# Late modulation products of a hybrid attention and mLSTM trunk, taken out of the attention steps and placed between tiles of the gate and branch projections

## The reference

```python
shift, scale, gate = jnp.split(mod, 3, axis=-1)          # mod = silu(c) @ w_mod + b_mod, 3 * 1024 wide
u = layer_norm(x) * (1.0 + scale) + shift
qa, ka, va, za, qm, km, vm, om, gm, zm, qw, kw, vw, zw, g_merge = split_columns(u @ w_in)
# A: grouped attention over all keys; C: windowed attention with a sink; B: bidirectional mLSTM
merged = sum(sigmoid(g_i) * ((y_i * silu(z_i)) @ w_branch[i]) for i in (A, B, C))
h = alpha * x + gate * (merged @ w_out)
x = layer_norm(h) * ln_g + ln_b
```

## Time and profile before

| | |
|---|---|
| median of three runs | 1557.13 us |
| span of the profiled execution, its own time | 1555.3 us |
| PE busy | 1519.7 us, 98% of the span |
| DVE, POOL, ACT busy | 48%, 40%, 30% |
| granted PE clock, mean | 0.998 of full speed |
| late products at L962 (`raw`) | 20.6 us busy, 3.2 us idle before them |
| C's attention steps up to the context scores, layer 0 | 64.87 us, with 24 pieces |
| the same in layer 1 | 52.16 us, with 8 pieces |

### The profile page before, as it was taken

How to read it: one execution, slowest core, us unless ns; L and a number is a source line. 1 busy time by engine, 2 the same in 40 slices (tenths; PEclk the granted TensorE clock), 3 DMA queues, 4 the chain that set the end, 5 groups by cost and what they waited for, 6 DMA issues and landing times.

```text
span 1555.3 us, 22672 instructions
## 1 busy us (share of the span) xinstructions
PE 1519.7 (98%) x9091; PEld 1248.3 (80%) x9091; DVE 743.9 (48%) x1467; ACT 473.8 (30%) x1099; POOL 629.2 (40%) x501
## 2 busy tenths in 40 slices
PE   8999999999999999999999999999999999999997
PEld 6798788885788887788878977889768888778886
DVE  5596710646423333622497584125680136262257
ACT  1246710155410123411144485012671003232010
POOL 3551045600145453145773401555104554423562
PEclk9999999999999999999999999999999999999999
DMA  9420022317222222025431100222311221211421
GB/s 339 114 72 29 1 68 68 108 60 244 69 68 82 68 68 61 28 77 180 121 127 42 58 15 14 68 82 82 100 41 55 81 82 55 68 49 44 173 81 68
DMA packets 80488, 128.72 MB, mean 83 GB/s; under 512 B 16444, under 2 KB 29184, under 8 KB 80384
## 3 DMA queue, kind: packets, MB, share of 16 engines
q1 hardware_dynamic: 78144, 122.03, 24.8%
q10 hardware_dynamic: 2240, 5.24, 0.9%
HBM read 120.96 MB, written 6.30 MB: 82 GB/s over the span
## 4 chain that ended last, share of the span: by engine, by line
PE 82%; DVE 8%; POOL 3%; ACT 2%; issue 2%; DMA 2%; SPq 0%; POOLq 0%; DVEq 0%; ACTq 0%
PE pb L1018 55%; PE pb L1163 5%; PE pb L1292 4%; PE pb L1043 3%; PE pb L1243 3%; PE pb L1206 2%; PE pb L962 1%; PE pb L1214 1%; PE pb L1473 1%; DMA raw<-in_w_mod 1%; PE pb L1336 1%; DVE ks L2138 1%; DMA raw<-in_w_in 1%; POOL slot_T L857 1%; ACT pr L1749 1%
## 5 line engine op out<-in xcount | busy, mean ns | idle before, releaser
L1018 PE MATMUL pb<-wsp,act_T 128*128 128x512 f32 x3048 | 713.5, 392 | 4.4 <-DVE act_T L2077 2.0
L1018 PEld LDWEIGHTS pb<-wsp,act_T 128*128 128x128 f32 x3048 | 568.3, 188 | 128.8 <-issue 7.1
L854 POOL CAST wsp<-raw 128x1024 fp32r<-128x1024 f32 x128 | 136.5, 1067 | 804.3 <-PE pb L1018 651.6
L857 POOL TENSOR_TENSOR wsp<-raw,wsp 128x512 fp32r<-128x512 f32 x268 | 360.2, 1365 | 10.2
L1018 PE MATMUL pb<-wsp,yT 128*128 128x512 f32 x720 | 165.7, 390 | 0.0
L1018 PEld LDWEIGHTS pb<-wsp,yT 128*128 128x128 f32 x720 | 135.1, 188 | 27.9
L2610 DVE SCALAR_TENSOR_TENSOR mt<-tg,pb 128x512 f32<-128x512 f32 x40 | 27.4, 686 | 216.6 <-PE pb L1018 215.8
L1903 ACT ACTIVATE tg<-pb 128x512 f32<-128x512 f32 x60 | 35.9, 599 | 275.9 <-PE pb L1018 275.9
L1749 ACT ACTIVATE pr<-pb,nm 128x640 f32<-128x640 f32 (+2 forms) x128 | 91.4, 714 | 2.5 <-DVE nm L2279 2.4
L1243 PE MATMUL pb<-ident,pr 128*128 128x128 f32 x480 | 73.7, 274 | 2.6 <-ACT pT L1784 2.3
L2309 DVE TENSOR_SCALAR pr<-pr,rden 128x640 f32<-128x640 f32 (+2 forms) x128 | 70.9, 554 | 4.5
(11 more groups left out here) (301 smaller groups left out, 1963.1 us busy)
## 6 DMA issues: line engine op xcount, KB each, us to landing
raw<-in_w_in SPq DMA_DIRECT2D x112, 512.0 KB, 3.4
raw<-in_w_mod SPq DMA_DIRECT2D x32, 512.0 KB, 4.3
raw<-in_w_branch SPq DMA_DIRECT2D x24, 512.0 KB, 3.6
raw<-in_w_out SPq DMA_DIRECT2D x16, 512.0 KB, 3.7
stage<-in_w_mod SPq DMA_DIRECT2D x28, 256.0 KB, 7.2
raw<-in_w_in SPq DMA_DIRECT2D x16, 256.0 KB, 5.4
xh<-in_x_sample SPq DMA_DIRECT2D x6, 512.0 KB, 5.9
out<-xh ACTq DMA_DIRECT2D x5, 512.0 KB, 2.9
```

The source lines that it names most:

```text
L854: pool.tensor_copy(hi, raw[:, p % 3, :, 0:width]).then_inc(raw_hi, 1)
L857: ins = pool.tensor_tensor(lo[:, j, :], raw[:, p % 3, j, 0:width], hi[:, j, :].bitcast(F32), ALU.subtract)
L1018: mm = pe.matmul(dst, lhs(a, k, t), w[:, wa, j, 0:width], start=(k == 0 and n == 0), stop=(i == count - 1 and j == 1 and n == 2))
```

## The change

The late chunks leave the attention steps of C. `late_sum(n)` makes the 32 products and 4 bias matmuls of a chunk in one run; a table `LATE_SUMS` says after which pass and tile of a projection it stands, and where the turned copies stand. Four chunks are done in or just behind branch A of layer 0 (the fourth in the q projection of C), two in the branch projections of C of layer 0, two in those of A of layer 1. The pieces get a ring of their own, `mod_raw`, of eight buffers, which lies over the attention's `qT` and `kT` and is therefore filled only after the context scores: SP waits for them ahead of eight of the loads, and the next weight piece is issued behind these. `gates()` moves to the start of branch B, and takes banks in turn as the late chunks now do, which shifts the banks of the projections behind them. The `raw` ring carries weights only.

```diff
-LATE_CHUNKS = (((1, 0), (1, 2), (1, 1), (1, 3), (0, 4), (0, 5)), ((1, 4), (1, 5)))
-
-MOD_AT = ((*range(2, 8), *range(10, 28)), (2, 4, 6, 8, 10, 12, 14, 16))
+LATE_CHUNKS = [(1, 0), (1, 2), (1, 1), (1, 3), (0, 4), (0, 5), (1, 4), (1, 5)]
+
+MOD_SLOTS = 8
+LATE_LOADS = {(0, "A"): {2: range(0, 8), 8: range(8, 12), 12: range(12, 16)},
+              (0, "C"): {2: range(16, 24)}, (1, "A"): {2: range(24, 32)}}
+LATE_SUMS = {(0, "A", "BR", 0, 0, 4): ("sum", 0), (0, "A", "BR", 0, 1, 2): ("turn", 0),
...
-                for n, (ll, c) in enumerate(LATE_CHUNKS[l]):
-                    if n == 1:
-                        add((br, "G", 0), "in", KD, (COL_G + BRANCH[br] * D, HALF), part=(0,))
-                    add(("gmod", ll, c), "mod", KD, (c * HALF, HALF), of=ll)
-                    if n == 1:
-                        add((br, "G", 0), "in", KD, (COL_G + BRANCH[br] * D, HALF), part=(1,))
...
+            for i in range(4):
+                psum.roll(("gate", i))
...
+        mod_raw = at("mod_raw", [P, MOD_SLOTS, 2, HALF], F32, arena + 46592)
...
+                def load_late(m):
+
+                    ll, c = LATE_CHUNKS[m // 4]
+                    if m >= MOD_SLOTS:
+                        sp.wait_ge(mod_used, m - MOD_SLOTS + 1)
+                    k = 2 * (m % 4)
+                    sp.dma_start(mod_raw[:, m % MOD_SLOTS, :, :],
+                                 w_mod[ll, k * P:(k + 2) * P, c * HALF:(c + 1) * HALF].rearrange("(k p) n -> p k n", p=P))\
+                        .then_inc(mod_in[m % MOD_SLOTS], 16)
...
                     load_piece(p)
+                    for br in ("A", "C"):
+                        n = p - pieces.first[l, (br, "G", 0)]
+                        for m in LATE_LOADS.get((l, br), {}).get(n, ()):
+                            if n == 2:
+                                wait_full(sp, (br, "Sctx"))
+                            load_late(m)
...
+                def late_sum(n):
+
+                    key, (ll, c) = ("gmod", n), LATE_CHUNKS[n]
+                    acquire(key)
+                    b = bank_of(key)
+                    for m in range(4 * n, 4 * n + 4):
+                        pe.wait_ge(mod_in[m % MOD_SLOTS], 32 + 16 * (m // MOD_SLOTS + 1))
+                        for k in range(2):
+                            mm = modulation(b, 2 * (m % 4) + k, mod_raw[:, m % MOD_SLOTS, k, :])
                         mm.then_inc(mod_used, 1)
+                    modulation_bias(b, ll, range(4 * c, 4 * c + 4)).then_inc(*full(key))
...
-                        if br == "C":
-                            late_step(s)
...
+                        def beside_gate(i, t):
+                            if hf == 0:
+                                between(i, t)
+                            late(l, br, "G", hf, i, t)
...
-                        project((br, "G", hf), after=None if hf else between)
+                        project((br, "G", hf), after=beside_gate)
...
+                elif l == 0:
+                    late_row(3)
                 q_path(br, 0)
+                if (l, br) == (0, "C"):
+                    late_columns(3)
```

More of the change, by code:

```diff
@@ L231, with late_banks @@
 O_BANKS = ((5, 5, 5, 5), (5, 6, 5, 2))
-def late_modulation(l, psum, s):
-    if s in MOD_AT[l][::4]:
-        n = MOD_AT[l].index(s) // 4
-        psum.take(("gmod", n), 6 + n % 2)
-    if s - 2 in MOD_AT[l][3::4]:
-        n = MOD_AT[l].index(s - 2) // 4
-        if LATE_CHUNKS[l][n][1] < 4:
-            psum.take(("gmodT", n), 6 + n % 2)
+def late_banks(psum, *place):
+    if place in LATE_SUMS:
+        what, n = LATE_SUMS[place]
+        if what == "sum":
+            psum.roll(("gmod", n))
+        else:
+            psum.roll(("gmodT", n))
 def plan_layer(l, pieces, psum):
@@ L290, in plan_layer @@
                         psum.roll((br, name, t))
+                    for n, t in ((n, t) for n in range(4) for t in range(T)):
+                        late_banks(psum, l, br, name, 0, n, t)
                     continue
@@ L362, in plan_layer @@
             i = BRANCH[br]
[L363 to L364 removed]
+            add((br, "G", hf), "in", KD, (COL_G + i * D + hf * HALF, HALF))
             add((br, "BR", hf), ("branch", i), BW // P, (hf * HALF, HALF))
@@ L368, in plan_layer @@
                     psum.roll((br, name, hf, t))
+                for n, t in ((n, t) for n in range(4) for t in range(T)):
+                    late_banks(psum, l, br, name, hf, n, t)
                 if br != "B" and (name, hf) == ("G", 0):
@@ L372, in plan_layer @@
                         psum.roll(key)
-                    if br == "C":
-                        for i in range(4):
-                            psum.take(("gate", i), psum.use[l, keys[i % 3]][0])
                 if (br, name, hf) == ("B", "G", 0):
@@ L1108, in gates, with late @@
                         mm.then_inc(*full(("gate", i)))
-                def late_step(s):
-                    chunks = LATE_CHUNKS[l]
-                    if s in MOD_AT[l]:
-                        n, i = divmod(MOD_AT[l].index(s), 4)
-                        ll, c = chunks[n]
-                        key = ("gmod", n)
-                        if i == 0:
-                            acquire(key)
-                        p = pieces.first[l, ("gmod", ll, c)] + i
-                        pe.wait_ge(raw_in[p % 3], pieces.loaded[p])
-                        for j in range(2):
-                            mm = modulation(bank_of(key), 2 * i + j, raw[:, p % 3, j, :])
-                        mm.then_inc(mod_used, 1)
-                        if i == 3:
-                            modulation_bias(bank_of(key), ll, range(4 * c, 4 * c + 4)).then_inc(*full(key))
-                    if s - 2 in MOD_AT[l][3::4]:
-                        n = MOD_AT[l].index(s - 2) // 4
-                        if chunks[n][1] < 4:
-                            turn_chunk(("gmodT", n), (4 if l == 0 else 0) + n)
+                def late_sum(n):
[6 more added lines that the diff above has]
+                            mm = modulation(b, 2 * (m % 4) + k, mod_raw[:, m % MOD_SLOTS, k, :])
+                        mm.then_inc(mod_used, 1)
+                    modulation_bias(b, ll, range(4 * c, 4 * c + 4)).then_inc(*full(key))
+                def late(*place):
+                    if place in LATE_SUMS:
+                        what, n = LATE_SUMS[place]
+                        if what == "sum":
+                            late_sum(n)
+                        else:
+                            wait_done(pe, ("gmod", n))
+                            turn_chunk(("gmodT", n), n)
                 def attention(br):
@@ L1134, in attention @@
                     if br == "C":
-                        project((br, "q"))
+                        project((br, "q"), after=lambda i, t: late(l, br, "q", 0, i, t))
                     def turned(what, t):
@@ L1318, in context @@
                             values_context()
-                        if br == "C" and (i, t) == (2, T - 1):
-                            gates()
                     return context
@@ L1502, in _ @@
                     if br == "B":
+                        gates()
                         mlstm()
@@ L2372, in attention, with late_row, late_columns @@
                     y_lo_context()
+                def late_row(n):
+                    if 2 <= n < 6:
+                        wait_full(dve, ("gmodT", n - 2))
+                    elif n >= 6:
+                        wait_full(dve, ("gate", 3), 0)
+                    take_row(("gmod", n), n)
+                def late_columns(n):
+                    take_columns(("gmodT", n), LATE_CHUNKS[n][1])
                 def mlstm():
```

59 lines of the change are left out of this document (24 added, 35 removed), and 5 rows, old and new, of the table LATE_SUMS.

## The result

The changed kernel takes 1562.84 us (median of eight runs, 1562.11 to 1564.34), the kernel before, run beside it, 1558.34 us (1556.05 to 1560.02). The ratio is 1.0032, with a 95% interval of 1.0022 to 1.0041: slower, by more than the 0.2% that can be told. The span is 1560.3 instead of 1555.3 us. The forecast, 1559.0 us and no change, was too low by 3.8 us, or by 3.1 us if the ratio is put on the median it was made from (1.0032 x 1557.13 = 1562.1). The range held the time.

The account below looks back on a forecast made before the run. PE, busy for 98% of the span, was taken as the bound. Runs 19.7 + copies 0.8 + bank wait 0.7 - give-back 19.3 = +1.9 us on 1557.13 gave 1559.0 us, range 1555.3 to 1563.0.

Parts of the forecast that it names:

- The runs: Eight moved chunks, each made in one run between projection matmuls at 2.46 us: 19.7 us in all.
- The copies: Four turned copies, each now alone between projection matmuls, cost 0.2 us each, 0.8 us in all.
- the wait for `wcb`: Columns of B, layer 0: PE's first transpose waits for ACT's read of o tile 4, 0.7 us once.
- I add 0.3 us for POOL's splits: C's first nine steps: POOL's splits put the start of step 9 at 12.9 us instead of 12.6.
- The stretch without splits: C's steps without pieces or splits: first nine 12.6 us, two periods of 12.63, last seven steps 10.70.
- The sign that the prediction had named for being wrong: C's first nine steps above 13.5 us, with stretched normalisations beside POOL's casts.
- The first rival: C's first steps: POOL's splits hold DVE instructions 0.7 us each; three uncovered holds give 1562.6 us; chance 0.16.
- The shifted turns matter at one place: PSUM banks: the shifted order costs a wait only at B's columns in layer 0, 0.7 us.
- The give-back: C's steps, freed of pieces, shrink from 64.87 and 52.16 us to 48.9: 16.0 and 3.3, together 19.3.
- The second rival: C's steps: without pieces, PE's 0.69 us of waits in each period vanish too, giving 1554.9 us; chance 0.12.
- The third: Rival: eight late-piece loads at once fall under 225 GB/s and PE waits; 1586 us at 128 GB/s; chance 0.02.
- The fourth: Rival: a run costs no less than pieces apart, 2.64 us, giving 1560.4 us; chance counted within the forecast's 0.70.

Follow-up runs that it names:

- experiment ten: Kernel before, C's first two gate pieces loaded behind the modulation pieces and split by POOL only after C's context scores: 1554.27 us, ratio 0.9973.
- experiments five to eight: Early splits, kernel before (span 1558.5 us); changed kernel: half late products (span -5.0), splits from unit 12 (span 1566.7), or unit 26, other banks, pieces between steps (time 1566.0).

## Why the prediction was wrong, point by point

**The mechanism was the one forecast, and what the change adds on PE was sized right.** The runs cost 8 x 2.455 = 19.6 us (19.7). The copies cost 0.5 (0.8), the wait for `wcb` 0.8 (0.7). The first two were read from rows of the same instructions in another place, the third from the read that it waits for.

**The step that failed first is "I add 0.3 us for POOL's splits".** The stretch without splits was forecast at 12.6 + 36.0 = 48.6 us and is 48.47. That it fits so well is luck: the first nine steps take 13.2 us, not 12.6, and of the two periods taken at 12.63 the first takes 11.91 and only the second 12.64. With the splits the stretch is 49.58: they cost 1.11 us a layer, not 0.3, and 1.6 us too little stands in the sum. The sign that the prediction had named for being wrong came, first nine steps above 13.5 us (14.3). The first rival had the mechanism and three held instructions; its price, 0.7 us for each, 2.1 for three, was too high, since 1.81 us of held DVE became 1.11 of stretch. It should have been a term of the sum, not a chance of 0.16: the order of POOL's work said that the splits would fall there, and A's rows showed the hold.

**The step that failed second is "The shifted turns matter at one place".** They matter at two. The bank of C's first gate tile in layer 1 was not followed, and it cost 1.3 us. The forecast of the span was +1.9 us. With 1.6 for the splits, 1.3 for the bank and -0.3 for the stretches without splits, -0.3 for the copies and +0.1 for `wcb` it is 4.3, and 4.5 was measured where the program changed; the remaining 0.5 of the 5.0 us has no edit near it. By layer, layer 0 lost 0.8 us where the program changed, "about even" as forecast, and layer 1 3.7 instead of 1.6.

**The give-back was read from a stretch that held other losses.** 64.87 and 52.16 us contained 3.3 and 0.4 us that went without a piece leaving the steps, and so were the splits' and the loads' (experiment ten). Cleared of them, 32 pieces between the steps cost 13.09 + 3.25 = 16.3 us and in runs 19.6 + 0.5. So taking them out costs 3.8 us; that the splits also moved, to a cheaper place, gave 3.75 - 2.23 = 1.5 back; the banks cost 2.2. The sum, 4.5 us, is that of the distances above.

**The second rival is refuted as a whole.** PE's waits went in one of its three periods a layer (steps 9 to 16, 11.91 us) and stayed in the other two (12.64 and 10.69); without splits a stretch leaves 4.1 us of PE unused. **The third** too: PE never waited for a piece of `mod_raw`. **The fourth**: a run costs 2.455 us, less than 2.64.

**A term that was set at nothing and was nothing:** the gates in front of B and the rows and columns on DVE show no wait.

## What to carry to other kernels

Before work is taken out of a stretch, ask what else the stretch was paying for: here the cheap edit was to move the splits of the helper engine, not the products. Small products between the steps of a latency-bound stage cost less than their length only where PE has gaps (0.23 us a piece in the first nine steps, 0.58 in the next eight, 0.61 in a run), so look for the gaps step by step, not in the mean. And when a stretch comes out longer than its waits explain, read the granted clock of that stretch before blaming the edit. After any shift in a round of PSUM banks, list for each tile the former user of its bank and when that is read, at every place and in every layer, not only where a wait stood before.

## What the runs showed of the hardware

- POOL's casts and subtractions held DVE's `tensor_tensor` and `tensor_scalar` instructions whatever their size, also those of 128x1: 0.16 became 0.92, 0.15 became 0.43 to 0.64, a normalisation of 0.42 or 0.49 became 1.20 to 1.39. The reductions from PSUM beside them kept their 0.55 and 0.68 us. The Trainium skill, SBUF — State Buffer, Who interferes with whom, says that VectorE and GpSimd share a pair of SBUF ports, that where both want it the one that comes second is blocked for the whole instruction of the other, and that `tensor_reduce` does not contend. The traces agree, and show that tiny operations are held as well.
- The price of the same two splits depends on the place. They cost 0.5 to 0.8 us at the start of A, 1.12 at the start of C, 3.45 in steps 9 to 16 of C without pieces, 1.74 later in its middle with pieces beside the first split, and 5.2 to 6.0 near its end, there with a part of the clock's.
- The granted clock fell from 1.00 to 0.50 (1.2 GHz) for some us after waits of PE of 0.6 to 2.0 us, mostly two or three close together (experiments five to eight), and eight value products went from 0.87 to 1.98 us. Like waits elsewhere, 0.78 and 1.03 us at the start of the changed kernel, left it at 1.00. Whole times go with it: in experiment ten the two runs with a mean clock of 0.997 took 1556.2 and 1556.4 us, the seven with 0.998 or 0.999 1553.3 to 1554.4.
- The stretches of a kernel's two layers agree within 0.02 us where their work is the same, and repeat in another kernel within 0.02 (48.46, 48.47, 48.47), while the time of a run varies by 2 us. A stretch between two instructions tells a microsecond that the whole time can't.
